# Block 1's third down unit, first norm, branch sums and first-unit rounding in another order on the vector, scalar and GpSimd engines

## The reference

```python
for l in range(DEPTH):                       # block 1
    h = _rmsnorm(x, g_mix[l])
    proj = h @ w_in[l]
    ...
    branch = jnp.einsum('bsnc,ncd->bsnd', ys, w_branch[l])
    gates = jax.nn.sigmoid(gate_pre.reshape(bsz, seq, N_BRANCH, D_MODEL) + gate_b[l])
    mixed = jnp.sum(gates * branch, axis=2)
    x = x + mixed @ w_out[l]
    x = x + _conv_ffn(_rmsnorm(x, g_ffn[l]), w_up[l], ffn_conv_w[l], ffn_conv_b[l], w_down[l])
for l in range(DEPTH):                       # block 2
    m_x = modulation(c, w_mod[l], b_mod[l])
    xs = ffn_half_step(xs, m_x, 0, ...); mixer; xs = ffn_half_step(xs, m_x, 2, ...)
return rmsnorm(xs, final_norm)
```

## Time and profile before

| | us |
|---|---|
| median of 3 runs | 2683.22 |
| lowest, highest | 2679.45, 2685.55 |
| the profiled execution | 2684.6 |
| its span in the profile | 2682.8 |
| PE busy, share of the span | 2574.2 (96%) |
| DVE busy | 1485.0 (55%) |
| ACT busy | 1029.1 (38%) |
| POOL busy | 69.8 (3%) |

### The profile page before, as it was taken

One profiled execution on the slowest core, in us unless ns is written; L12 is line 12 of the kernel. 1 busy time (PEld: TensorE's weight loads), 2 busy tenths in 40 slices (PEclk: granted clock), 3 DMA queues, 4 the chain that ended last, 5 costly groups with the idle time before them and its releaser, 6 DMA issues.

```text
span 2682.8 us, 47374 instructions
## 1 busy us (share of the span) xinstructions
PE 2574.2 (96%) x19893; PEld 2248.9 (84%) x19893; DVE 1485.0 (55%) x2131; ACT 1029.1 (38%) x1395; POOL 69.8 (3%) x81
## 2 busy tenths in 40 slices
PE   7998999999899999999999999999999999998999
PEld 6998999899899978888776678888788888866999
DVE  6777785777778553333535564333443343545655
ACT  4544564545456432222324432122231222444433
POOL 3003000000200000000000000000000000000000
PEclk8999999999999999999999999999999999998999
DMA  8577766666676652432426542332352433554573
GB/s 225 167 238 180 215 173 175 213 204 206 188 205 169 180 155 69 121 96 76 148 80 198 158 126 79 102 110 70 113 140 75 121 85 92 169 166 127 148 197 110
DMA packets 613845, 393.61 MB, mean 147 GB/s; under 512 B 47470, under 2 KB 609428, under 8 KB 613539
## 3 DMA queue, kind: packets, MB, share of 16 engines
q1 hardware_dynamic: 610623, 383.31, 49.2%
q0 software_dynamic: 2176, 6.42, 1.1%
q10 hardware_dynamic: 868, 1.31, 0.2%
HBM read 389.94 MB, written 1.05 MB: 146 GB/s over the span
## 4 chain that ended last, share of the span: by engine, by line
PE 87%; DVE 6%; ACT 3%; issue 2%; POOL 1%; DMA 1%; DVEq 1%; ACTq 0%; SPq 0%; POOLq 0%
PE acc L964 12%; PE acc L965 11%; PE acc L966 11%; PE scores L964 6%; PE scores L965 6%; PE scores L966 6%; PE scores L1005 3%; PE scores L1006 3%; PE scores L1007 3%; PE acc L1005 3%; PE acc L1006 3%; PE acc L1007 3%; PE stat L1132 2%; DVE wlo L1969 2%; ACT whi L1459 1%
## 5 line engine op out<-in xcount | busy, mean ns | idle before, releaser
L1459 ACT ACTIVATE whi<-raw 128x2048 fp32r<-128x2048 f32 (+3 forms) x337 | 568.1, 1687 | 854.0 <-PE acc L966 257.6
L1969 DVE TENSOR_TENSOR wlo<-raw,whi 128x2048 fp32r<-128x2048 f32 (+2 forms) x315 | 653.6, 2075 | 240.4 <-ACT whi L1459 240.0
L964 PE MATMUL acc<-h_hi,whi 128*128 128x256 f32 (+1 forms) x2052 | 659.5, 321 | 12.1 <-DVE u L2500 3.5
L965 PE MATMUL acc<-h_lo,whi 128*128 128x256 f32 (+1 forms) x2052 | 651.6, 318 | 0.0
L966 PE MATMUL acc<-h_hi,wlo 128*128 128x256 f32 (+1 forms) x2052 | 651.3, 317 | 0.0
L964 PEld LDWEIGHTS acc<-h_hi,whi 128*128 128x128 f32 x2052 | 387.4, 189 | 49.4 <-issue 9.8
L965 PEld LDWEIGHTS acc<-h_lo,whi 128*128 128x128 f32 x2052 | 387.6, 189 | 28.4 <-issue 1.2
L966 PEld LDWEIGHTS acc<-h_hi,wlo 128*128 128x128 f32 x2052 | 387.4, 189 | 27.2
L964 PE MATMUL scores<-h_hi,whi 128*128 128x256 f32 (+1 forms) x960 | 319.7, 333 | 1.2 <-DVE wlo L1969 0.9
L965 PE MATMUL scores<-h_lo,whi 128*128 128x256 f32 (+1 forms) x960 | 318.0, 331 | 0.0
L966 PE MATMUL scores<-h_hi,wlo 128*128 128x256 f32 (+1 forms) x960 | 317.9, 331 | 0.0
(11 more groups left out here) (304 smaller groups left out, 3480.4 us busy)
## 6 DMA issues: line engine op xcount, KB each, us to landing
raw<-in_ffn_w_in_dram SPq DMA_DIRECT2D x176, 512.0 KB, 5.0
raw<-in_w_mod_dram SPq DMA_DIRECT2D x72, 1024.0 KB, 5.1
raw<-in_w_in_dram SPq DMA_DIRECT2D x62, 1024.0 KB, 5.8
raw<-in_w_up_dram SPq DMA_DIRECT2D x88, 512.0 KB, 5.1
raw<-in_ffn_w_out_dram SPq DMA_DIRECT2D x64, 704.0 KB, 4.7
raw<-in_w_down_dram SPq DMA_DIRECT2D x32, 704.0 KB, 4.7
raw<-in_w_out_dram SPq DMA_DIRECT2D x16, 1024.0 KB, 6.8
raw<-in_w_branch_dram SPq DMA_DIRECT2D x16, 512.0 KB, 7.3
```

The source lines that it names most:

```text
L964: pe.matmul(bank, wh, hi[:, c0 + k, 0:width], start=(k == 0), stop=False)
L965: pe.matmul(bank, wh, lo[:, c0 + k, 0:width], start=False, stop=False)
L1459: return act.activation(out_, in_, ACT.Copy, **kw)
L1969: dve.tensor_tensor(wlo[:, s % 2, 0:el], raw[:, slot, 0:el], f32(whi[:, s % 2, 0:el]), ALU.subtract).then_inc(s_lo, 1)
```

## The change

It does six things. (1) At the start, POOL makes no `wlo`: ACT rounds the first unit in two halves behind all squares, DVE makes its first half before and its second half within the scaling of the chunks (`first_low`), and the second unit is rounded and split in halves within it too. (2) The first weight unit behind every norm (`behind_norm`) is rounded and split as two halves. (3) The branch sums go by pairs: for branches 1 and 2 POOL adds pairs 0 to 2 and DVE pair 3; for the last one POOL adds pairs 0 and 1, DVE pairs 2 and 3. (4) ACT rounds the second out unit before it rounds the sums. (5) The third down unit is rounded before the last SiLU, and its `wlo` made before the last `a_lo`, `af`, `a_lo`. (6) The load of `cstage` waits for 8 units of up more.

```diff
@@ class Phase
+        self.behind_norm = name[1] == "." and name[3:] in ("." + "glu", ".up", ".ffn1.up0", ".in", ".ffn2.up0")
@@ POOL
-            pool.wait_ge(s_head_hi, 1)
-            first_low(0, 0).then_inc(s_head_lo, 1)
-            pool.wait_ge(s_head_hi, 2)
-            first_low(1, 0)
-            pool.wait_ge(s_lo, 1)
-            pool.wait_ge(s_hi, 2)
-            first_low(1, 1).then_inc(s_lo, 1)
+            pool.wait_ge(s_lo, 2)
...
-                for j in range(1, BRANCHES - 1):
+                for j in range(1, BRANCHES):
                     more = DC * BRANCH_ORDER[j]
-                    for m in range(0, DC, 4):
-                        pool.wait_ge(s_accfree, ph.t0 + DC * j + m + 4)
+                    for q in range(3 if j < BRANCHES - 1 else 2):
+                        pool.wait_ge(s_accfree, ph.t0 + DC * j + 2 * q + 2)
                         if j > 1:
-                            pool.wait_ge(s_mix, 7 * l + m // 4 + 1)
...
+                            pool.wait_ge(s_mix, 8 * l + 3 * (j - 2) + q + 1)
...
-            pool.wait_ge(s_accfree, by_name[f"1.{DEPTH - 1}.up"].t0)
+            pool.wait_ge(s_accfree, by_name[f"1.{DEPTH - 1}.up"].t0 + 16)
             pool.dma_start(cstage[:, :, :], A["ctx_2"][0].rearrange("(t p) d -> p t d", p=P)).then_inc(s_cx, 16)
@@ ACT, round_next
+                if e == 0 and to.behind_norm:
+                    half = el // 2
+                    copy(whi[:, s % 2, 0:half], raw[:, slot, 0:half]).then_inc(s_half, 1)
+                    copy(whi[:, s % 2, half:el], raw[:, slot, half:el]).then_inc(s_hi, 1)
+                    return
@@ ACT, the start
-                if c == 2:
-                    first_high(0, 0)
             n("sum", 8)
+            act.wait_ge(s_raw[0], phases[0].landed[0])
+            half = phases[0].el // 2
+            for part in range(2):
+                cols = slice(part * half, part * half + half)
+                copy(whi[:, 0, cols], raw[:, 0, cols]).then_inc((s_half, s_hi)[part], 1)
+            take_root(norm_x(1, ("g_mix", 0), h1_hi, h1_lo))
             turned_rows(blocks_turned[0])
-            first_high(0, 1)
-            first_high(1, 0)
-            take_root(norm_x(1, ("g_mix", 0), h1_hi, h1_lo))
-            first_high(1, 1)
...
+                def second_unit(e):
+
+                    if e in (3, 5):
+                        round_second(phases[0], e // 2 - 1)
+
+                round_norm(norm_x(1, ("g_mix", l), h1_hi, h1_lo), None if l else second_unit)
@@ ACT, behind the branches
                 for j in range(BRANCHES):
                     round_next(nm + "branch", j, None)
+                round_next(nm + "out", 0, None)
                 for q in range(DC // 2):
-                    if q < 3:
-                        act.wait_ge(s_mix, 7 * l + 5 + q)
+                    if q < 2:
+                        act.wait_ge(s_mix, 8 * l + 7 + q)
                     else:
-                        act.wait_ge(s_mixlast, l + 1)
+                        act.wait_ge(s_mixlast, 2 * l + q - 1)
@@ ACT, behind up
                 j = FC
+                round_next(nm + "down0", 1, None)
                 act.wait_ge(s_accfree, ph.t0 + 2 * FC)
                 act.activation(sg1[:, (j - 1) % 2, :], cg[:, (j - 1) % 2, :], ACT.Silu).then_inc(s_silu, 1)
...
-                        for j in range(1, DC):
+                        for j in range(2, DC):
                             round_next(nm + "down0", j, None)
@@ DVE, the start
-            dve.wait_ge(s_hi, 1)
-            dve.wait_ge(s_head_lo, 1)
-            dve.tensor_tensor(wlo[:, 0, half:2 * half], raw[:, 0, half:2 * half], f32(whi[:, 0, half:2 * half]),
-                              ALU.subtract).then_inc(s_lo, 1)
             flatten(norm_x(1, ("g_mix", 0), h1_hi, h1_lo))
+            dve.wait_ge(s_half, n("half", 1))
+            dve.tensor_tensor(wlo[:, 0, 0:half], raw[:, 0, 0:half], f32(whi[:, 0, 0:half]), ALU.subtract).then_inc(s_head_lo, 1)
+
+            def first_low(e):
+
+                if e == 1:
+                    dve.wait_ge(s_hi, 1)
+                    dve.tensor_tensor(wlo[:, 0, half:2 * half], raw[:, 0, half:2 * half], f32(whi[:, 0, half:2 * half]),
+                                      ALU.subtract).then_inc(s_lo, 1)
+                if e in (4, 6):
+                    rest_second(phases[0], e // 2 - 2)
@@ DVE, the branches
-                        if j == BRANCHES - 1 and q == 3:
-                            dve.wait_ge(s_mix, 7 * l + 4)
+                        if j and j < BRANCHES - 1 and q == 3:
                             settle()
-                            dve.tensor_tensor(total(q), total(q), gate, ALU.add).then_inc(s_mixlast, 1)
+                            dve.tensor_tensor(total(q), total(q), gate, ALU.add)
+                for q in range(2, 4):
+                    c = DC * BRANCH_ORDER[-1] + 2 * q
+                    if q == 2:
+                        dve.wait_ge(s_mix, 8 * l + 6)
+                    settle()
+                    dve.tensor_tensor(total(q), total(q), gates[:, c:c + 2, :], ALU.add).then_inc(s_mixlast, 1)
@@ DVE, behind up
+                rest_next(nm + "down0", 1, None)
                 dve.wait_ge(s_ahi, FC * l + FC - 1)
                 rest_a(FC - 2, None)
```

## The result

| | before | changed |
|---|---|---|
| median, us | 2683.22 | 2666.88 |
| lowest, highest | 2679.45, 2685.55 | 2665.49, 2670.53 |
| ratio to before, 95% interval | | 0.9946, 0.9935 to 0.9958 |
| profiled span | 2682.8 | 2663.7 |

The change takes 16.3 us off by the medians. The forecast was 2662.5 with a range of 2656 to 2672: the sign and the range hold, the size is 4.4 us too large.

A forecast was written before the change was run, and what follows sets the result against it. PE, busy 96% of the span, was taken as the bound, so gains come from its pauses and half clock: 4.2 + 4.8 + 3.3 + 3.4 + 6.0 = 21.7, giving 2662.9 or 2661.5; 2662.5 was taken, range 2656 to 2672.

The forecast's parts named there:

- The start: Term 1, first two units: PE starts at 18.5 instead of 26.33, glu ends 5.9 us earlier, 4.2 us gained at nav.
- what is late next? The load of nav: Step of term 1, behind glu: nav's load lands at 44.5, nav can start at 48.9, so PE waits 2.4 us there.
- 2.4 if the last parameter rows land late: Lower bound of term 1: the start gains 2.4 us, not 4.2, if the rows land late or the pause costs half clock.
- The sums and the second out unit: Term 2, branch sums and out, both layers: out starts 1.5 us sooner, the 0.82 and 0.79 waits go; 2.4 a layer, 4.8.
- out's first unit: Step of term 2: PE starts out at 251.2 and needs the second out unit's `wlo` at 258.2.
- The halves: Term 3, first unit behind a norm: 0.65 us sooner at five sites 256 columns wide, 3.3 us in all.
- the chain behind it, down to the last `h_lo`, is DVE's own: Step of term 3, behind the split at a norm: the split ends 0.7 us sooner, so PE gets 0.65.
- The context rows: Term 4, layer 1's modulation units and up: loading 1 MB later removes held-up PE code and half clock, 3.4 us.
- The third down unit: Term 5, layers 0 and 1: pauses of 2.17 and 2.26 go, and layer 0's half clock behind; 6.0 us.
- the start gives nothing: Rival, chance 0.14: nav's or dilq's load comes 4 us later than put, term 1 is nothing; 2667, with half clock 2670.
- The adds get in each other's way: Rival, chance 0.12, branch sums: POOL and DVE take turns, POOL winning each; term 2 falls from 4.8 to 2; 2665.5.
- pause stays: Rival, chance 0.08, layer 1's modulation units: the pause of 3.65 has another cause and stays, term 4 goes; 2666.

## Why the prediction was right, and where its sizes were not

**The start** was forecast at 4.2 and gave 2.8 (1.1 when alone). The step that failed is "what is late next? The load of nav". Up to glu the working was near: DVE's first half ended at 16.2 instead of 14.7, because `root` stands ahead of it and waited for PE's sum of squares until 14.68, so PE started at 19.43 instead of 18.5 and glu ended at 34.5 instead of 33.6. But the last parameter rows landed at 36.6. The bound "2.4 if the last parameter rows land late" named it; it should have been the value taken. The SP timeline of the kernel before had the row for it: the last small load goes out just before nav's load.

```profile
29.71 1.06 SPq L808 DMA_DIRECT2D prow<-in_final_norm_dram  x1
```

POOL's transfers lie in its way. They did not move forward by 0.7 us, as the prediction has it: the table is issued at 26.94 in the changed kernel and was at 26.67 before. Nav's load landed at 45.1, where 44.5 was forecast, and ACT waited 0.85 for it; but its split was done at 49.3 and PE came to nav only at 50.34, so nothing was lost there.

```profile
45.09 1.92 ACT L1443 ACTIVATE whi<-raw 128x2048 fp32r<-128x2048 f32 x1 [0.85 <-DMA raw<-in_w_in_dram]
```

**The sums and the second out unit** were forecast at 2.4 a layer and gave 1.5. The mechanism of the sums held: the 0.82 and the 0.79 went, and out started 1.8 sooner, where 1.5 was forecast. The term that was mis-sized is out's first unit, 7.0 us in the prediction (251.2 to 258.2); it took 8.23. The Trainium skill, "Perfetto Trace Analysis", section "Optimizing Scalar/DVE Operations", has it that moving work between GpSimd and DVE might not help, since they share a port. The trace agrees with the port and not with the outcome: two of DVE's `wlo` take 2.79 where 2.28 is their time (rows below), and out still starts sooner.

DVE in the changed kernel, a `wlo` beside POOL's adds, the two last adds, the four `h_lo`:

```profile
234.62 2.79 DVE L1966 TENSOR_TENSOR wlo<-raw,whi 128x2048 fp32r<-128x2048 f32 x1
...
245.58 1.81 DVE L2370 TENSOR_TENSOR gates<-gates 128x512 f32<-128x512 f32 x2
247.31 2.49 DVE L2349 SCALAR_TENSOR_TENSOR h_lo<-gates,h_hi 128x512 fp32r<-128x512 f32 x4
```

What the sum had not counted is the clock: the 6.8 us at half clock behind out's start where 3.4 stood before, worth 1.1 a layer. The prediction left the 3.4 as they were and gave no reason. The run with this part alone shows that pauses of the same length, 4.44 and 4.45, are followed by 6.8 in one layer and 3.4 in the other, and the kernels with the old sums show that 6.8 was common there too, but hidden by the 0.79.

**The halves** were forecast at 0.65 a site and gave 0.2 to 0.4 at four of the narrow ones, some 1.7 in all instead of 3.3. The step that failed is "the chain behind it, down to the last `h_lo`, is DVE's own": ACT's half of the second unit, which waits for PE, stands in it. Block 2's first feed-forward, with 0.36 to 0.74, is the one site that comes near 0.65.

**The context rows** were forecast at 3.4 and gave 3.5 from the modulation units to the third up unit, with the mechanism as told.

**The third down unit** was forecast at 6.0 and gave 5.9 alone by the medians; in the changed kernel 2.3 and 1.7 at half clock in layer 0, and 2.4 less 0.65 in layer 1. The fourth unit's split was put at 885.2 and PE's need at 886.2; it was late by 0.65, behind the copies of `xc`.

Measured against the forecast: 1.4 less at the start, 1.8 less at the sums, 1.6 less for the halves, 0.2 less at the down unit, together 5.0; the median lies 4.4 above it. The agreement is partly luck, since the half clock in block 2, which nobody moved, gave 1.5 in the pair of profiles.

Of the rivals, "the start gives nothing" was half true by another transfer than the one it named. "The adds get in each other's way" gave the right time, 2665.5, by the wrong mechanism. "Start gives nothing" (2667) and "pause stays" (2666) lie as near to 2666.9, so the time alone can't choose among them; the rows do. The parts alone add up to 11.2 us by their medians and the whole is 16.3; each has an interval of some 2.5 us on either side, so this doesn't show that they need each other. By the ratios it is 8.9 and 14.5.

What stays open: why one pause is followed by 3.4 us at half clock and an equal one by 6.8, and how long the last parameter rows would take with no other transfer at all; neither was tried. That out's half clock is felt more once the `wlo` wait is gone is read from the rows, not from a run made for it.

## What to carry to other kernels

A pause of PE of some microseconds costs itself and the half clock behind it. If it can't be shortened, matmuls that nobody needs, put into it, took some 4 us off here (2.5 in each layer by the rows). A wait that goes can also lay bare a half clock that it had hidden. When a stall at the start is removed, list every transfer that is due in the next 20 us with the issue and the landing of its last piece, the small ones too, and not just the weight load that waits longest today. When an engine is late and its work is split so that it begins sooner, look at the next instruction on it that waits for another engine, for there the gain ends.

## What the runs showed of the hardware

The granted clock of the same instructions at the same place is not a property of the kernel. The changed kernel was profiled twice: once PE's first units had 6.8 us at half clock from 18.2, the other time none until 3.4 us from 37.6. All profiled executions together had 24.0 to 61.4 us at half clock, the start of PE's first unit at half clock in some and at full clock in others, and in the middle of the program the stretches were 3.4, 6.8 or 13.7 us long. In the kernel with the sums alone, 3.4 us more of it behind out cost 1.1 us (8.12 against 7.02).

The instruction queue moves packets of 16 KB, which we take for PE's code. In the five kernels with the context rows at the old place, the one that PE needed started only when that transfer of 1 MB was nearly through, 4.8 to 5.1 us after its issue. PE went on 1.2 to 1.4 us after the packet's end.

The last row of parameters, 4 KB, was in use 5.1 to 6.4 us after its issue with the table in its way (three kernels), and 7.0 to 8.6 us after it (28.6 to 36.7 in the changed kernel) with the table and the bias windows (six kernels).

Beside POOL's adds of 128x512, DVE's `wlo` of 128x2048 took 2.79 us instead of 2.28; beside adds of 128x1024 it took 4.25.
